# Query projection in three tiles for four heads, the rotary rows put in place by transfers

## The reference, cut to what matters

```python
def mla_mixer(h, w_dq, q_g, w_uq, w_dkv, kv_g, w_ukv, w_o):
    cq = rms_norm(h @ w_dq, q_g)                                   # (512, 256)
    q = (cq @ w_uq).reshape(bsz, s, 16, 64 + 32)
    q_nope, q_rope = q[..., :64], q[..., 64:]
    ckv = h @ w_dkv
    ...
    q_rope = apply_rope(q_rope, cos[:, None, :], sin[:, None, :])  # x1*cos - x2*sin, x2*cos + x1*sin
    k_rope = apply_rope(ckv[..., 256:], cos, sin)                  # one rotary key for all heads
    ...
        logits = (jnp.einsum('bqhd,bkhd->bhqk', q_nope[:, q0:q1], k_nope[:, :kend])
                  + jnp.einsum('bqhr,bkr->bhqk', q_rope[:, q0:q1], k_rope[:, :kend]))
```

## Time and profile before

| | us |
|---|---|
| median of 3 runs | 1083.61 (1083.59 to 1083.78) |
| the profiled execution | 1083.48 |
| its span | 1081.7 |
| PE busy | 1068.1 |
| DVE / ACT / POOL busy | 810.6 / 473.5 / 225.1 |

### The profile page before, as it was taken

One profiled execution on the slowest core, in us unless ns is written; L12 is line 12 of the kernel. 1 busy time (PEld: TensorE's weight loads), 2 busy tenths in 40 slices (PEclk: granted clock), 3 DMA queues, 4 the chain that ended last, 5 costly groups with the idle time before them and its releaser, 6 DMA issues.

```text
span 1081.7 us, 18501 instructions
## 1 busy us (share of the span) xinstructions
PE 1068.1 (99%) x6626; PEld 947.6 (88%) x6626; DVE 810.6 (75%) x1112; ACT 473.5 (44%) x698; POOL 225.1 (21%) x209
## 2 busy tenths in 40 slices
PE   8999999999999999999999999999999999999997
PEld 7888888999999998888878766789999999978887
DVE  5655659999999999444557688599999999984343
ACT  6212236644444446222346477465444444552222
POOL 6000001323322320111200255013332232101110
PEclk9999999999999999999999999999999999999999
DMA  7333242233333233333322102113233323332321
GB/s 198 98 96 116 79 117 78 79 117 96 98 116 108 86 107 109 114 97 99 103 97 67 42 21 59 39 40 118 92 102 116 105 89 116 107 107 81 106 66 78
DMA packets 144038, 101.65 MB, mean 94 GB/s; under 512 B 3913, under 2 KB 142337, under 8 KB 144001
## 3 DMA queue, kind: packets, MB, share of 16 engines
q1 hardware_dynamic: 143648, 100.61, 30.7%
q0 software_dynamic: 320, 0.55, 0.2%
q10 hardware_dynamic: 32, 0.01, 0.0%
HBM read 99.06 MB, written 2.10 MB: 94 GB/s over the span
## 4 chain that ended last, share of the span: by engine, by line
PE 93%; DVE 2%; ACT 2%; issue 1%; DMA 1%; SPq 0%; DVEq 0%; ACTq 0%
PE ps L376 28%; PE ps L377 28%; PE ps L378 28%; PE ps L1613 3%; PE ps L1674 2%; PE ps L1690 2%; ACT hid_hi L758 1%; DMA x_nat<-in_x 1%; DVE op_w_lo L524 1%; PE ps L436 0%; PE ps L1655 0%; PE ps L1657 0%; PE ps L1656 0%; DVE w_sum L1035 0%; PE ps L1749 0%
## 5 line engine op out<-in xcount | busy, mean ns | idle before, releaser
L376 PE MATMUL ps<-x_op_hi,op_w_hi 128*128 128x256 f32 x1232 | 349.2, 283 | 1.7 <-DVE op_w_lo L524 1.7
L377 PE MATMUL ps<-x_op_lo,op_w_hi 128*128 128x256 f32 x1232 | 348.6, 283 | 0.0
L378 PE MATMUL ps<-x_op_hi,op_w_lo 128*128 128x256 f32 x1232 | 348.6, 283 | 0.0
L376 PEld LDWEIGHTS ps<-x_op_hi,op_w_hi 128*128 128x128 f32 x1232 | 236.4, 192 | 3.4 <-DVE op_w_lo L524 2.1
L377 PEld LDWEIGHTS ps<-x_op_lo,op_w_hi 128*128 128x128 f32 x1232 | 236.5, 192 | 0.1
L378 PEld LDWEIGHTS ps<-x_op_hi,op_w_lo 128*128 128x128 f32 x1232 | 236.5, 192 | 0.0
L376 PE MATMUL ps<-hid_hi,wgt_hi 128*128 128x512 f32 (+1 forms) x550 | 211.6, 385 | 1.4 <-DVE wgt_lo L360 1.4
L378 PE MATMUL ps<-hid_hi,wgt_lo 128*128 128x512 f32 (+1 forms) x550 | 209.5, 381 | 0.0
L377 PE MATMUL ps<-hid_lo,wgt_hi 128*128 128x512 f32 (+1 forms) x550 | 209.4, 381 | 0.0
L360 DVE TENSOR_TENSOR wgt_lo<-raw,wgt_hi 128x1024 fp32r<-128x1024 f32 (+4 forms) x131 | 137.4, 1066 | 90.8 <-ACT wgt_hi L351 89.2
L351 ACT ACTIVATE wgt_hi<-raw 128x1024 fp32r<-128x1024 f32 (+4 forms) x131 | 106.9, 831 | 150.3 <-PE ps L378 148.7
(11 more groups left out here) (163 smaller groups left out, 1220.7 us busy)
## 6 DMA issues: line engine op xcount, KB each, us to landing
pair_raw<-in_ffn_w_gate SPq DMA_DIRECT2D x22, 1024.0 KB, 5.3
pair_raw<-in_ffn_w_up SPq DMA_DIRECT2D x22, 1024.0 KB, 5.3
raw<-in_conv_w_in SPq DMA_DIRECT2D x24, 512.0 KB, 3.9
raw<-in_ffn_w_down SPq DMA_DIRECT2D x32, 384.0 KB, 3.4
raw<-in_ffn_w_down SPq DMA_DIRECT2D x32, 320.0 KB, 2.9
raw<-in_conv_w_out SPq DMA_DIRECT2D x8, 512.0 KB, 3.7
raw<-in_mla_w_o SPq DMA_DIRECT2D x8, 512.0 KB, 3.8
x_nat<-in_x SPq DMA_DIRECT2D x4, 512.0 KB, 7.3
```

Source lines behind the costliest of these rows:

```text
L376: nc.tensor.matmul(acc, wh, xh, start=first, stop=False)
L377: nc.tensor.matmul(acc, wh, xl, start=False, stop=False)
L378: return nc.tensor.matmul(acc, wl, xh, start=False, stop=last)
```

## The change

The query projection makes three tiles for four heads where it made four. Tile 0 of a group holds the 32 rotary rows of four heads; tiles 1 and 2 hold the plain rows of two heads each. `q_tile(g, t)` takes the place of `q_head`; the 12 tiles alternate between banks 6 and 7 as the heads did.

DVE multiplies tile 0 once with cosines and once with sines into `q_turned` (`rotate(g)`, two operations for four heads). SP then issues eight transfers (`spread_rope(g)`), which put 32 rows each into `q_even` and `q_odd`. ACT copies the plain rows out of PSUM (`nope_copies(pair)`, two operations for a pair of heads). The signs and the exchange of halves are now in the key: `k_T` holds the rotated key, and in the other 32 rows the key with exchanged halves. `k_T` gets these rows by two SP transfers of 64 x 8 x 512 numbers (1 MB each) in place of the four copies. Odd heads have the rotary rows in rows 0 to 63 and the plain ones in rows 64 to 127.

```diff
+            def spread_rope(g):
+
+                sp.wait_ge(q_rot, g + 1)
+                for k in range(GROUP):
+                    hd = GROUP * g + k
+                    first = (NOPE, 0)[hd % 2]
+                    for n in range(2):
+                        sp.dma_start(q_Ts[hd % 2][first + n * ROPE:first + (n + 1) * ROPE, hd // 2, :],
+                                     q_turned[k * ROPE:(k + 1) * ROPE, g % 2, n, :]).then_inc(q_rope_in[g], 16)
+
             for name in shape:
                 ub, n = shape[name][0:2]
+                if name == "q_up":
+                    sp.wait_ge(w_used, U0["latent"] + 2 * LC + 1)
+                    sp.wait_ge(k_rope_done, 1)
+                    for par in range(2):
+                        rows_to = slice(NOPE, P) if par == 0 else slice(0, 2 * ROPE)
+                        sp.dma_start(k_T[rows_to, par::2, :],
+                                     k_rope[NOPE:P, :].unsqueeze(1).broadcast_to([2 * ROPE, PAIRS, S])).then_inc(k_rope_in, 16)
                 for u in range(2 if name == "conv_in" else 0, ub):
...
                     load_unit(sp, name, 0, u)
+                    if name == "q_up" and u:
+                        for g in (u - 1, u) if u == ub - 1 else (u - 1,):
+                            spread_rope(g)
...
-            for u in range(2, 4):
-                prepare(sc, unit_hi, "kv_up", 0, u)
+
+            def nope_copies(pair):
+
+                if pair % 2:
+                    sc.wait_ge(w_used, U0["q_up"] + pair // 2 + 1)
+                else:
+                    sc.wait_ge(q_prod, pair + 2)
+                for par in range(2):
+                    own = slice(64 * par, 64 * par + NOPE)
+                    ins = nc.scalar.activation(q_Ts[par][own, pair, :], ps[own, q_bank(pair // 2, 1 + pair % 2), :], ACT.Copy)
+                ins.then_inc(q_nope, 1)
...
-            def rotate(hd):
+            def rotate(g):
+
+                ve.wait_ge(q_prod, 2 * g + 1)
+                if g == 0:
+                    ve.wait_ge(q_tables_in, 32)
+                elif g == 1:
+                    ve.wait_ge(k_rope_in, 32)
+                else:
+                    ve.wait_ge(q_rope_in[g - 2], 2 * GROUP * 16)
+                acc = ps[:, q_bank(g, 0), :]
+                nc.vector.tensor_tensor(q_turned[:, g % 2, 0, :], acc, q_cos[:, :], ALU.mult)
+                nc.vector.tensor_tensor(q_turned[:, g % 2, 1, :], acc, q_sin[:, :], ALU.mult).then_inc(q_rot, 1)
...
-            def q_head(hd):
+            def q_tile(g, t):
...
+                n = 3 * g + t - 2
+                if n >= 0:
+                    if n % 3 == 0:
+                        pe.wait_ge(q_rot, n // 3 + 1)
+                    else:
+                        pe.wait_ge(q_nope, 2 * (n // 3) + n % 3)
                 for c in range(LC):
...
             def logits(hd):

-                pe.wait_ge(q_out, hd + 1)
+                if hd % 2 == 0:
+                    pe.wait_ge(q_nope, hd // 2 + 1)
+                if hd % GROUP == 0:
+                    pe.wait_ge(q_rope_in[hd // GROUP], 2 * GROUP * 16)
...
-            for hd in range(8):
-                q_head(hd)
+            for g in range(2):
+                for t in range(3):
+                    q_tile(g, t)
```

More of the change, by code:

```diff
@@ L209, in trunk_kernel @@
         mask, _, e = place("mask", [P, S], F32, e)
+        q_sin, _, e = place("q_sin", [P, S], F32, e)
         assert e <= HID_END
@@ L213, in trunk_kernel @@
         c_q, _, e2 = place("c_q", [P, LC, S], F32, e2)
-        rope, _, e2 = place("rope", [P, S], F32, e2)
+        q_cos, _, e2 = place("q_cos", [P, S], F32, e2)
         assert e2 <= HL_END
+        k_own, _, e2 = place("k_own", [P, S], F32, FREE_LO)
+        k_other, _, e2 = place("k_other", [P, S], F32, e2)
+        assert e2 <= e
+        q_turned, _, _ = place("q_turned", [P, 2, 2, S], F32, TMP)
         prob_T, _, e = place("prob_T", [P, 1, L_COLS], F32, e)
@@ L254, in trunk_kernel @@
         k_prod, k_out, v_prod, v_out = sem("k_prod"), sem("k_out"), sem("v_prod"), sem("v_out")
-        k_rope_early, k_rope_late = sem("k_rope_early"), sem("k_rope_late")
-        q_prod, q_out = sem("q_prod"), sem("q_out")
+        k_rope_in, q_tables_in = sem("k_rope_in"), sem("q_tables_in")
+        q_prod, q_nope, q_rot = sem("q_prod"), sem("q_nope"), sem("q_rot")
+        q_rope_in = [sem(f"q_rope_in{g}") for g in range(GROUPS)]
         s_prod, s_read, exp_done = sem("s_prod"), sem("s_read"), sem("exp_done")
@@ L454, in norm_rows, with q_bank @@
             nc.scalar.activation(inv[:, :], inv[:, :], ACT.Exp, scale=-0.5).then_inc(inv_ready, 1)
[L456 to L462, removed]
+        def q_bank(g, t):
+            return 6 + (3 * g + t) % 2
         def v_count(n):
@@ L580, in latents @@
             pool.dma_start(mask[:, :], consts[:, P:P + S]).then_inc(tables_in, 16)
-            pool.dma_start(rope[:, :], consts[:, P + S:P + 2 * S]).then_inc(tables_in, 16)
+            for n, table in enumerate((k_own, k_other)):
+                pool.dma_start(table[NOPE:P, :], consts[NOPE:P, P + (n + 3) * S:P + (n + 4) * S]).then_inc(tables_in, 16)
+            for n, table in enumerate((q_cos, q_sin)):
+                pool.dma_start(table[:, :], consts[:, P + (n + 1) * S:P + (n + 2) * S]).then_inc(q_tables_in, 16)
         @block.gpsimd
@@ L865, in k_copy @@
                 for par in range(2):
-                    ins = nc.scalar.activation(k_T[0:NOPE, 2 * n + par, :], ps[64 * par:64 * par + NOPE, n % 4, :], ACT.Copy)
+                    own = slice(64 * par, 64 * par + NOPE)
+                    ins = nc.scalar.activation(k_T[own, 2 * n + par, :], ps[own, n % 4, :], ACT.Copy)
                 ins.then_inc(k_out, 1)
@@ L870, in _ @@
                 k_copy(n)
[L871 to L874, removed]
+                if n == 1:
                     latent_rows(1)
             latent_hi(1, "q_norm")
-            k_rope_part(nc.scalar.copy, 1).then_inc(k_rope_early, 1)
             for u in range(2):
@@ L881, in _ @@
                 k_copy(n)
-            for u in range(2, 4):
-                prepare(sc, unit_hi, "kv_up", 0, u)
+            def nope_copies(pair):
[4 more added lines that the diff above has]
+                for par in range(2):
+                    own = slice(64 * par, 64 * par + NOPE)
+                    ins = nc.scalar.activation(q_Ts[par][own, pair, :], ps[own, q_bank(pair // 2, 1 + pair % 2), :], ACT.Copy)
+                ins.then_inc(q_nope, 1)
+            nope_copies(0)
+            prepare(sc, unit_hi, "kv_up", 0, 2)
+            nope_copies(1)
+            nope_copies(2)
+            prepare(sc, unit_hi, "kv_up", 0, 3)
+            nope_copies(3)
             def exponentials(hd, n):
@@ L906, in _ @@
             exponentials(0, 0)
+            nope_copies(4)
             exponentials(0, 1)
+            nope_copies(5)
             exponentials(1, 0)
@@ L910, in _ @@
             front_copy(0)
+            nope_copies(6)
+            nope_copies(7)
             for i in range(1, PAIRS):
@@ L1350, in _ @@
             rotate(1)
+            prepare(ve, unit_lo, "kv_up", 0, 3)
+            row_low(0)
             rotate(2)
[L1352 to L1357, removed]
             factors(0)
-            rotate(10)
             row_low(1)
-            rotate(11)
             factors(1)
+            rotate(3)
             back_copies(0)
-            rotate(12)
-            rotate(13)
             for i in range(1, PAIRS):
                 row_low(2 * i)
-                if i == 1:
-                    rotate(14)
                 if i >= 2:
```

88 lines of the change are left out of this document (39 added, 49 removed).

## The result

The changed kernel takes **1094.91 us** (median of 4 runs, 1094.60 to 1095.32) against 1083.61: ratio 1.0104, 95% interval 1.0093 to 1.0116. That is 11.3 us slower, where 6.3 were forecast.

A forecast was written before the change was run, and what follows sets the result against it. PE's work and whether PE is kept fed were taken as the bound. Removed matmuls -5.4 us and waits +11.7 made +6.3 on 1083.48; with the median 0.1 above that run, 1089.9 us, range 1087.3 to 1094.

The forecast's parts named there:

- The sign and the place: Slower by 6.3 us, slower given 0.93; PE standing before tile (1,1) for 6.4 us and tile (2,1) for 4.1.
- Two rounds of 'eight issues, a load, a split' lie in series: SP's third and fourth `q_up` loads wait behind transfers, and splits hold up copies and rotations; each round 6.8 us.
- The term of -5.4: Sixteen heads become twelve tiles on PE: 24 matmuls of 0.227 us fewer, if nothing waits.
- SP's issues start 0.45 apart: eight are 3.6: Price in us of the eight SP transfers issued ahead of the third and of the fourth `q_up` load.
- It costs nothing then, which I take: PE's clock drops to 1.2 GHz in the first wait; slow tiles fit into 4.1 us to spare before the second.
- rival (b): PE's low clock reaches the path, by slow pieces or a second fall: +1.5 to +4 us, 1091 to 1094; chance 0.14.
- I take the full rate: The key's transfers inside SBUF run at 330 GB/s, so the first two `q_up` units land by 576.1.
- estimate of 580.5: Landing of the first two `q_up` units if the key's transfers run at the skill's 196 GB/s; still in time.
- The 0.8 us of room: Slack for the second `q_up` unit's landing before DVE's first value copy, at the skill's transfer rate, in place of 5.
- Rival (c): Slow key's transfers hold up the second `q_up` unit: +1 us at half rate, 1104 at a quarter; chance 0.10.
- turn(0)'s wait of 0.7: PE waits 0.7 us for `turn(0)` at 614.8, behind `nope_copies(4)`, exponentials, two reciprocals and POOL's 2.05.
- Rival (d): Not slower: small transfers issue and land almost at once, eight issues at 0.1 us each, giving 1082; chance 0.10.

The follow-up runs named there:

- Experiment 1: Changed kernel with SP issuing all four `q_up` loads ahead of the eight-transfer groups: 1081.17 us, ratio 0.9975 to the kernel before.
- experiment 5: Changed kernel, SP's order kept, ACT's and DVE's splits of the third and fourth `q_up` units moved behind copies and rotations that PE and SP need: 1084.00 us.
- experiment 3: Changed kernel with the third and fourth `q_up` loads issued after four of the eight transfers instead of after all: 1089.39 us.
- experiment 8: Changed kernel: four `q_up` loads ahead of the eight-transfer groups, two ahead of the key's; `rotate(3)` ahead of `factors(1)`; ACT's and DVE's late splits moved back: 1079.03 us.
- Experiment 4: Kernel before the change plus four batches of unneeded transfers behind the `q_up` loads, from SBUF or HBM, 32 or 128 rows: 1083.37 us, one execution.
- experiment 2: Changed kernel with matmuls nobody reads, 30 ahead of tile (1,1) and 20 ahead of tile (2,1), keeping PE busy: 1093.54 us.
- experiment 6: Kernel before the change plus four unused transfers, one at a time, 64 or 128 rows, inside SBUF or from HBM: 1084.11 us, one execution.

## Why the prediction was right in kind and short in size

**The sign and the place were right.** "Two rounds of 'eight issues, a load, a split' lie in series" is what the trace shows, at the two tiles named, ended by the copies named. Experiment 1 shows the load's place to be the cause (-13.7 us), experiment 5 that the other half is the work in line behind the split (-10.9), experiment 3 that the length goes with the number of issues ahead of the load.

**The term of -5.4 was right**: PE's work between the same two points fell to 32.2 in experiment 8, with 0.46 of waiting ahead of `logits(0)` and some short waits without a bracket, like the one ahead of tile (0,2); 31.3 was forecast for no wait at all.

**The step that failed first** is "SP's issues start 0.45 apart: eight are 3.6". They took 5.07 and 5.05, a miss of 1.45 in each round, 2.9 us in all. I had priced an issue that the profile of before doesn't contain (source in SBUF) by one that it does (source in HBM), and gave it a range of 0.37 to 0.5 as if the spread of the known rows were the doubt about the unknown kind. Experiment 4 gives 0.62 to 0.64 for one of this kind. With 3.5 instead of 3.2 for the landing (0.3 a round) that is 3.5; by the table the two rounds are 3.1 longer. The three splits on the way give back the rest: they took 0.96 (ACT, 597.37 to 598.33), 0.94 (DVE, 598.34 to 599.28) and 0.96 (ACT, 609.20 to 610.16) where the stamps had 1.0, 1.1 and 1.1, 0.35 less in all.

**The second** is "It costs nothing then, which I take" of the clock. That was right of the first low stretch (0.14 at tile (1,1), 0.31 at tile (2,1) by experiment 2) and wrong of the whole: the clock fell again behind the second wait, on the path, for about 1.6 in the trace (5.22 against 3.6) and 1.4 in the medians of experiment 2. I had named this as rival (b), "if it fell again in the second wait", and given it 0.14. Where the rounds were shorter (experiments 3 and 5) there was no second fall; whether that is why isn't shown.

**The key's transfers**: "I take the full rate" was wrong. They ran at 166 to 198 GB/s. The rule of the Trainium skill that I had set beside it (SBUF — State Buffer, section on the DMA port swizzle, 196 GB/s for 64 partitions, measured there on 0 to 63, which reach as many ports as 64 to 127) fits this trace, and the estimate of 580.5 made from it for the landing meets the 580.84 of ACT's first split. It fits less well in experiment 6, where 64 rows out of HBM moved 215 and 256 GB/s in two slices.

The price was small all the same. DVE's timeline of the changed kernel, from the key's scaling to `rotate(0)`:

```profile
564.57 0.69 DVE L1322 TENSOR_TENSOR k_rope<-k_rope,inv 64x512 f32<-64x512 f32 x1
...
587.52 0.69 DVE L1349 TENSOR_TENSOR q_turned<-ps,q_cos 128x512 f32<-128x512 f32 x1 [0.67 <-PE ps L388]
```

Before, the first rotation began 587.12 - 564.42 = 22.70 behind the scaling; here it is 587.52 - 564.57 = 22.95. So 0.25 of the 0.4 at tile (0,0) came in between, and the other 0.15 was there before the transfers. Experiment 8, where the first two loads go ahead of the key's transfers, is back at 587.70 - 565.03 = 22.67; the versions with the transfers first have 22.88 to 23.34. The 0.8 us of room that I had counted was not there: I put two splits of 1.0 between the landing and 583.4, but DVE's first split waits for ACT's, so it is 2.9 (580.84 to DVE's copy at 583.72, before 583.28), and PE's next value product starts 0.14 late (584.46, 0.37 behind the one before). Rival (c) had the right rate and, with +1, too high a price.

**The small terms**: turn(0)'s wait of 0.7 did not appear. I had put POOL's whole 2.05 behind the second reciprocal, but POOL scales in two pieces, and only the second stands there:

```profile
616.12 0.93 POOL L679 TENSOR_SCALAR prob<-prob,small 128x384 f32<-128x384 f32 x2 [0.77 <-DVE small L1378]
```

It ends at 617.05 and `turn(0)` starts at 619.46; nor is it the low clock that hides a wait, since in experiment 2 at full clock `turn(0)` starts at 617.52 right behind tile (3,0). Tile (3,2) waited 1.3 by the starts (1.16 in the bracket) where 0.6 was forecast. That the two cancel is luck. Tile (0,2) has its 0.2: it starts 0.41 behind the matmul before it (588.45 to 588.86) in place of 0.227.

Sum: 6.3 forecast, 2.9 for the issues, 0.6 for the landings, 1.6 for the clock and 0.4 for the later tile (0,0), less 0.35 for the splits, make 11.45 against 11.3 measured; the rest is less than the spread between the executions (1094.60 to 1095.32).

**Rival (d)**, small transfers that issue almost at once, is refuted by the same rows: 0.62 to 0.64 each.

## What to carry to other kernels

Before a transfer is put on a queue, write down which load it delays and what stands in line behind that load's first reader: here the order of the queues, not the work, decided between +11.3 and -4.6 us. Price an operation that the profile doesn't show by its own kind (here by where its source lies) and, if no row has that kind, make the range wider than the spread of the rows that you have. When a wait is long enough to let the clock fall, look for the next wait too: the first fall may be free and the second on the path.

## What the runs showed of the hardware

- In a row SP issues transfers whose source lies in SBUF 0.62 to 0.64 us apart, with 32 rows as with 128 (experiment 4, batches one and three), and transfers out of HBM 0.44 apart (batch four). There are exceptions that I can't place: the `q_up` load right behind eight transfers out of SBUF took 0.58, the 640 KB of experiment 6 out of HBM 0.64, one issue of experiment 4 1.32, and the first two `q_up` loads of the changed kernel, behind the key's transfers, 5.65 together. Whether the issue ahead, or what is still in flight, has to do with it wasn't tried.
- The clock fell from 1.00 to 0.50 with PE already busy again, about a microsecond after a wait of 2.47 us, in a kernel in which it had been low until some 7 us before. A wait of 2.32 in experiment 5, with no low stretch before it, did not bring it down. Whether it is the length or what went before that decides, these runs don't tell.
- Two transfers of 1024 KB inside SBUF with 64 rows each moved 166 to 198 GB/s; 1280 KB inside SBUF over all 128 rows moved 285 to 317 (experiment 6).
